# Seven products for both column pairs of a feed-forward down projection, and the squared ReLU moved to ScalarE

## The chip, the core and the metric

The kernel runs on one core of one Trainium2 chip. The metric is the device time of one execution in microseconds (us). It is written in Bass: each engine (TensorE, VectorE, ScalarE, GpSimd, and SyncE, which issues most of the loads) has its own instruction list, worked through strictly in order, and the lists are tied together by semaphores. An instruction that waits holds up everything behind it in its list.

## What is computed

Two layers of an encoder trunk on 256 tokens of width 2048, all in f32. Each layer has a mixing half (an input projection, eight attention heads, a pooling group, an output projection) and a feed-forward half. The change touches the feed-forward half only:

```
x = x + RMSNorm(mix)
f = square(relu(RMSNorm(x) @ w_up)) @ w_down        # 2048 -> 8192 -> 2048
x = x + RMSNorm(f)
```

## The kernel before, in words

**Three products for one.** Every f32 operand is split into a rounded part and a remainder of the type fp32r: `w_hi` is a copy of the weights on ScalarE (`split_hi`, L956), `w_lo` the subtraction raw - w_hi on VectorE (`split_lo`, L1356). A product is then hi*hi + hi*lo + lo*hi, three matmuls of 128x128 weights and 512 columns (function `three`, L847 to L849). SyncE loads 128x1024 pieces of a weight matrix (512 KB each) into the four slots of `raw`; a slot is loaded again once its `w_lo` has been made. The split pieces go into a ring of eight slots, `w_hi` and `w_lo`; a slot is filled again after TensorE has used it (semaphore `w_used`). Four slots are a half, and halves alternate.

**The feed-forward half** works in four groups of 2048 hidden features per layer. A group has four up units (u = 0 to 3) and then the down stage, which adds the group's part to `acc` in two column pairs, j = 0 (output columns 0 to 1023) and j = 1 (the rest). A column pair takes 16 weight pieces in the order `K_ORDER`. Groups 0 to 2 do both pairs in `down_wide`. In the last group j = 0 is done there, and the columns of j = 1 as two plain units, partly loaded into `raw_side`.

**An up unit** leaves its result in `acc_pair[b]` (b = 0, 1), two banks of PSUM each, in which the first 256 columns of a bank hold one partial result and the second 256 another. TensorE works in four quarters: b = 0 and b = 1 on the first half of the weights, then b = 0 and b = 1 on the second, so b = 0 stands a quarter before the unit ends. VectorE adds the partial results with one reduce (L1822) into `act_f`, which frees the banks (semaphore `acc_free[b]`), and makes max(z, 0)*z (L1827). ScalarE copies that to `f_hi` (L1248), VectorE makes `f_lo` (L1833).

**The seven products.** In j = 0, at 4 of the 8 pairs of pieces (`SEVEN_AT`), the 2x2 block product is made with 7 block products instead of 8 (function `seven`, L852). It needs sums of token blocks (`s_sum`, made in up units 1 and 2, split to `s_hi` and `s_lo`), and sums of weight blocks: VectorE makes three into `t_sum` and one in place in `raw` (L1901 to L1913), ScalarE copies `t_hi` (L1263), and VectorE makes `t_lo` (L1917), which lies on the same memory as `t_sum`. So the sums of the next seven wait for `t_used`, which TensorE signals after each of the three products that read `t_hi` and `t_lo`. Three of the seven products go straight to banks of `acc_pair`; four go to banks of their own, the shared banks `ssa_bank`, `t_bank[0]`, `t_bank[1]` and `o_bank`, because they belong to several outputs. One seven is 21 matmuls, and the two plain pieces that follow it are 24. Before the change, the shared banks gather over all four groups of a layer, and `combine` adds them to `acc` in the last group.

**Order of VectorE.** The order is written out by hand. `seven_lo(g, n, ...)` makes the weight sums, two splits, `t_lo`, and two splits more. `wide_sums(g, j)` (L1843, L1846) are four closing sums from the banks of `acc_pair` into `acc`, each of which frees its bank; I call them the closing sums. TensorE starts the next stage when `acc_free` of the bank pair says so. In j = 0 the list is: the last two sevens, two splits of the next stage's first half, the closing sums, then splits. In j = 1 it is: 14 splits (two halves of its own, all of the next stage's first half, two slots of the second), the closing sums, two splits. ScalarE's list has the `w_hi` copies in the same order.

## Time and profile before

| | us |
|---|---|
| median of 3 runs (1904.0 to 1904.77) | 1904.55 |
| span of the profiled execution | 1903.1 |
| TensorE busy (matmul) | 1891.0 (99%) |
| VectorE busy | 1445.1 (76%) |
| ScalarE busy | 983.1 (52%) |
| GpSimd busy | 117.6 (6%) |
| loaded and stored | 380.79 MB, mean 200 GB/s |

The span goes from the first to the last instruction of one execution. The profile gives no other time for that execution; the median of the runs is 1.45 us above its span. The profile names engines PE (TensorE, its matmuls; PEld are its weight loads), DVE (VectorE), ACT (ScalarE), POOL (GpSimd) and SP (SyncE). A line such as `w_lo<-raw,w_hi` reads: writes w_lo, reads raw and w_hi. Matmuls overlap, so the duration of one (380 ns) is longer than the distance from one to the next.

### The profile page before, as it was taken

How to read it: one execution, taken by the hardware profiler on the slowest of the kernel's cores; microseconds unless marked ns; L12 is line 12 of the kernel's file. 1: busy time of each engine (PE TensorE's matmuls, PEld its weight loads, DVE VectorE, ACT ScalarE, POOL GpSimd, SP SyncE). 2: the span in 40 equal slices, each digit the busy share in tenths (PEclk: the TensorE clock that was granted, in tenths of full speed). 3: DMA queues.
4: the chain of work that ended last, by engine and by line, in shares of the span. 5: the costliest groups of instructions: out<-in, count | busy, mean ns of one | idle time of the engine just before them, and what ended most of it. 6: DMA issues, size and time to landing. Idle time of an engine off the chain costs nothing.

```text
span 1903.1 us, 28366 instructions
## 1 busy us (share of the span) xinstructions
PE 1891.0 (99%) x10022; PEld 1685.3 (89%) x10022; DVE 1445.1 (76%) x1777; ACT 983.1 (52%) x1285; POOL 117.6 (6%) x166
## 2 busy tenths in 40 slices
PE   9999999999999999999999999999999999999998
PEld 7988888988988998898888888889889889989987
DVE  6886768886796688579878757678767966876887
ACT  6455656554445445445554556555544544454443
POOL 3920020000000000000000000200000000000000
PEclk9999999999999999999999999999999999999999
DMA  8665356567558557666576554565766575576563
GB/s 290 203 223 173 118 190 218 181 200 241 183 175 262 178 175 227 215 199 187 210 242 220 180 166 138 183 213 169 234 216 200 187 241 187 172 241 209 184 225 149
DMA packets 168325, 380.79 MB, mean 200 GB/s; under 512 B 11968, under 2 KB 14128, under 8 KB 167728
## 3 DMA queue, kind: packets, MB, share of 16 engines
q1 hardware_dynamic: 167904, 377.58, 61.6%
q10 hardware_dynamic: 336, 2.11, 0.3%
q8 instruction: 49, 0.80, 0.2%
q14 instruction: 36, 0.29, 0.0%
HBM read 377.55 MB, written 2.10 MB: 199 GB/s over the span
## 4 chain that ended last, share of the span: by engine, by line
PE 94%; DVE 3%; DMA 1%; issue 1%; ACT 1%; POOL 0%; DVEq 0%; POOLq 0%; ACTq 0%; SPq 0%
PE acc_pair L548 25%; PE acc_pair L553 13%; PE acc_pair L514 8%; PE acc_pair L848 8%; PE acc_pair L516 8%; PE acc_pair L847 8%; PE acc_pair L515 8%; PE acc_pair L849 8%; DVE w_lo L1356 1%; PE o_bank L766 1%; PE t_bank L849 1%; PE t_bank L848 1%; PE t_bank L847 1%; DVE h_both L1410 1%; DMA raw<-in_w_down 0%
## 5 line engine op out<-in xcount | busy, mean ns | idle before, releaser
L1356 DVE TENSOR_TENSOR w_lo<-raw,w_hi 128x1024 fp32r<-128x1024 f32 x687 | 832.3, 1233 | 251.9 <-ACT w_hi L956 243.2
L956 ACT CAST w_hi<-raw 128x1024 fp32r<-128x1024 f32 x687 | 705.5, 1049 | 503.3 <-DVE raw L1904 119.3
L548 PE MATMUL acc_pair<-h_both,w_hi 128*128 128x512 f32 x2176 | 560.2, 380 | 0.1
L548 PEld LDWEIGHTS acc_pair<-h_both,w_hi 128*128 128x128 f32 x2176 | 371.1, 190 | 30.3 <-ACT proj L1025 0.5
L553 PEld LDWEIGHTS acc_pair<-h_both,w_lo 128*128 128x128 f32 x2176 | 327.4, 190 | 29.1
L553 PE MATMUL acc_pair<-h_both,w_lo 128*128 128x256 f32 x2176 | 330.4, 274 | 0.0
L847 PE MATMUL acc_pair<-w_hi,f_hi 128*128 128x512 f32 x672 | 254.7, 379 | 0.0
L848 PE MATMUL acc_pair<-w_lo,f_hi 128*128 128x512 f32 x672 | 254.7, 379 | 0.0
L849 PE MATMUL acc_pair<-w_hi,f_lo 128*128 128x512 f32 x672 | 254.7, 379 | 0.0
L514 PE MATMUL acc_pair<-w_hi,h_both 128*128 128x512 f32 x444 | 170.5, 384 | 1.7 <-DVE w_lo L1356 1.5
L515 PE MATMUL acc_pair<-w_lo,h_both 128*128 128x512 f32 x444 | 168.3, 379 | 0.0
L516 PE MATMUL acc_pair<-w_hi,h_both 128*128 128x512 f32 x444 | 168.3, 379 | 0.0
L514 PE MATMUL acc_pair<-w_hi,f_hi 128*128 128x512 f32 x384 | 148.2, 386 | 0.2
L1248 ACT CAST f_hi<-act_f 128x512 fp32r<-128x512 f32 x60 | 37.1, 619 | 214.1 <-DVE act_f L1827 214.1
L515 PE MATMUL acc_pair<-w_lo,f_hi 128*128 128x512 f32 x384 | 145.5, 379 | 0.0
L516 PE MATMUL acc_pair<-w_hi,f_lo 128*128 128x512 f32 x384 | 145.5, 379 | 0.0
L849 PEld LDWEIGHTS acc_pair<-w_hi,f_lo 128*128 128x128 f32 x672 | 127.0, 189 | 18.1
L848 PEld LDWEIGHTS acc_pair<-w_lo,f_hi 128*128 128x128 f32 x672 | 127.0, 189 | 18.0
L847 PEld LDWEIGHTS acc_pair<-w_hi,f_hi 128*128 128x128 f32 x672 | 127.0, 189 | 18.0
L1822 DVE TENSOR_REDUCE act_f<-acc_pair 128x512 f32<-128x1024 f32 x60 | 73.3, 1221 | 47.1 <-PE acc_pair L553 46.4
L2084 POOL TENSOR_TENSOR rstd<-mean_sq,minus_half 128x1 f32<-128x1 f32 (+1 forms) x16 | 13.5, 843 | 1421.9 <-DVE ss_post L1371 1149.4
L514 PEld LDWEIGHTS acc_pair<-w_hi,h_both 128*128 128x128 f32 x444 | 83.9, 189 | 16.1 <-issue 3.4
(245 smaller groups left out, 1905.4 us busy)
## 6 DMA issues: line engine op xcount, KB each, us to landing
raw<-in_w_up SPq DMA_DIRECT2D x256, 512.0 KB, 4.5
raw<-in_w_down SPq DMA_DIRECT2D x240, 512.0 KB, 4.9
raw<-in_w_in SPq DMA_DIRECT2D x128, 512.0 KB, 4.7
raw<-in_w_out SPq DMA_DIRECT2D x64, 512.0 KB, 5.4
raw_side<-in_w_down SPq DMA_DIRECT2D x16, 512.0 KB, 7.6
x<-in_x SPq DMA_DIRECT2D x8, 256.0 KB, 7.7
w_pool_s<-in_w_pool SPq DMA_DIRECT2D x2, 1024.0 KB, 7.4
post_row<-in_g_mix_post SPq DMA_DIRECT2D x2, 1024.0 KB, 7.4
```

What stands on the lines that cost most here:

```text
L514: pe.matmul(bank[:, :], xh, wh, start=begin and k == 0, stop=False)
L515: pe.matmul(bank[:, :], xh, wl, start=False, stop=False)
L516: mm = pe.matmul(bank[:, :], xl, wh, start=False, stop=end and k == 1)
L548: pe.matmul(acc_pair[b][:, m, :], w_hi[:, slot, col:col + P], x_both.rearrange("p s (a n) -> p s n a", a=2), start=(slot, k) == (0, 0), st ...
L553: mm = pe.matmul(acc_pair[b][:, m, 0:SEQ], w_lo[:, slot, col:col + P], x_hi.rearrange("p (a n) -> p n a", a=2), start=False, stop=(slot, k ...
L847: pe.matmul(bank, xh, in_turn(wh), start=start, stop=False)
L848: pe.matmul(bank, xh, in_turn(wl), start=False, stop=False)
L849: return pe.matmul(bank, xl, in_turn(wh), start=False, stop=stop)
L956: act.copy(w_hi[:, half * PAIRS + p, :], raw[:, p, :]).then_inc(hi_made, 1)
L1248: act.copy(f_part(f_hi, u, b), act_f[:, b, :].rearrange("p (k n) -> p k n", k=2)).then_inc(fhi_made, 1)
L1356: dve.tensor_tensor(w_lo[:, slot, :], src[:, p, :], w_hi[:, slot, :].bitcast(F32), ALU.subtract).then_inc(lo_made, 1)
L1822: dve.tensor_reduce(act_f[:, b, :].rearrange("p (k a n) -> p k a n", k=2, a=2), acc_pair[b][:, :, :].rearrange("p k (s n a) -> p k a n s", ...
```

## The change

In groups 0 to 2, j = 1 also uses seven products in 4 of its 8 pairs of pieces, with the same `K_ORDER` as j = 0. `SHARED` is 4. The shared banks no longer gather over the groups: every column pair starts them anew, and after each pair VectorE takes the four banks into `kept_sums` (`shared_sums`), which lies on the memory of `x`; `x` is therefore written to a tensor in HBM in group 0 and read back in the last group. `combine` is now done once for each j, for j = 1 in the up units of the last group. In the up units ScalarE copies the second halves of the banks to `act_f` (`take_half`), VectorE adds the first halves (`turned_sum`), and ScalarE does Relu, Square and the copy to `f_hi`.

On TensorE:

```diff
+                def bank_free(t, c, j, result):
+                    pe.wait_ge(acc_free[t], result + (c if j else 1))
-                def seven(g, n, hu, result):
+                def seven(g, j, n, hu, result):
-                    pe.wait_ge(flo_made, l * 32 + g * 8 + k1 // 2 + 1)
-                    pe.wait_ge(s_lo_made, no + 1)
+                    if j == 0:
+                        pe.wait_ge(flo_made, l * 32 + g * 8 + k1 // 2 + 1)
+                        pe.wait_ge(s_lo_made, (l * FF_GROUPS + g) * len(SEVEN_AT) + n + 1)
+                    if first and not (isinstance(g, int) and l + g + j == 0):
+                        pe.wait_ge(shared_free, shared_done(l, g, j))
                     pe.wait_ge(lo_made, (hu + i // PAIRS) * PAIRS + 2 + RAW)
                     three(ssa_bank[:, :], sh[:, 2, :], sl[:, 2, :], w_hi[:, s0, right],
-                          w_lo[:, s0, right], p_first, p_last)
+                          w_lo[:, s0, right], first, end)
...
                     for i in range(SLOTS):
-                        slot, kt = i % RING, K_ORDER[j][i]
-                        if j == 0 and i in SEVEN_AT:
-                            seven(g, SEVEN_AT.index(i), hu, result)
-                        if j == 0 and i - i % 2 in SEVEN_AT:
+                        slot, kt = i % RING, K_ORDER[i]
+                        if i in SEVEN_AT:
+                            seven(g, j, SEVEN_AT.index(i), hu, result)
+                        if i - i % 2 in SEVEN_AT:
                             continue
```

On ScalarE:

```diff
+                def take_half(g, u, b):
+                    result_stands(act, b, a0 + ACC_F + g * 8 + u,
+                                  hu0 + HU_F + g * HU_GROUP + u * 2 + 1)
...
+                    act.copy(act_f[:, b, :].rearrange("p (k a n) -> p k a n", k=2, a=2),
+                             acc_pair[b][:, :, SEQ:].rearrange("p k (n a) -> p k a n", a=2)
+                             ).then_inc(half_taken, 1)
                 def turned_hi(g, u, b):
+                    act.wait_ge(acc_free[b], 1 + a0 + ACC_F + g * 8 + u + 1)
+                    act.activation(act_f[:, b, :], act_f[:, b, :], ACT.Relu).then_inc(relu_made, 1)
+                    act.wait_ge(relu_made, turned_no(l, g, u, b) + 1)
+                    act.activation(act_f[:, b, :], act_f[:, b, :], ACT.Square).then_inc(f_ready, 1)
                     act.wait_ge(f_ready, l * 32 + g * 8 + u * 2 + b + 1)
...
+                        act.wait_ge(x_ready, l * 16 + 16)
+                        for t in range(T):
+                            act.dma_start(x_kept[l, t], x[:, t, :]).then_inc(x_saved, 16)
...
+                            if last and u == CHUNKS - 1:
+                                act.wait_ge(q_step, 16 * l + 8)
+                                act.dma_start(x[:, 0, :], x_kept[l, 0]).then_inc(x_back[0], 16)
...
-                    for k, bank in ((0, t_bank[0]), (1, t_bank[1])):
-                        act.copy(halves(q_sum[:, k, :]), put_back(bank[:, :])).then_inc(p_copied, 1)
...
-                    act.wait_ge(q_step, 8 * (l + 1))
+                    act.wait_ge(q_step, 16 * (l + 1))
+                    act.dma_start(x[:, 1, :], x_kept[l, 1]).then_inc(x_back[1], 16)
```

On VectorE:

```diff
-                def turned_square(g, u, b):
-                    dve.tensor_reduce(act_f[:, b, :].rearrange("p (k a n) -> p k a n", k=2, a=2),
-                                      acc_pair[b][:, :, :].rearrange("p k (s n a) -> p k a n s",
-                                                                     s=2, a=2),
-                                      AX.X, ALU.add).then_inc(acc_free[b], 1)
-                    dve.wait_ge(acc_free[b], 1 + a0 + ACC_F + g * 8 + u + 1)
-                    dve.scalar_tensor_tensor(z, z, 0.0, z, ALU.max, ALU.mult
-                                             ).then_inc(f_ready, 1)
+                def turned_sum(g, u, b):
+                    dve.wait_ge(half_taken, turned_no(l, g, u, b) + 1)
+                    z = act_f[:, b, :].rearrange("p (k a n) -> p k a n", k=2, a=2)
+                    dve.tensor_tensor(z, acc_pair[b][:, :, 0:SEQ].rearrange("p k (n a) -> p k a n", a=2),
+                                      z, ALU.add).then_inc(acc_free[b], 1)
+                def f_stands(g, u, b):
+                    dve.wait_ge(f_ready, l * 32 + g * 8 + u * 2 + b + 1)
...
+                    if between is not None:
+                        between()
                     split_lo(hu, half, (2, 3))
...
+                def shared_sums(g, j, first):
+                    if first and j == 0:
+                        dve.wait_ge(x_saved, 16 * T * (l + 1))
+                    dve.wait_ge(t_used, 3 * seven_no(l, g, j, len(SEVEN_AT)) - 1)
+                    for k, bank in enumerate((ssa_bank, t_bank[0], t_bank[1], o_bank)):
+                        dst = kept_sums[:, 1 - j, k, :]
+                        if first:
+                            dve.tensor_copy(dst, bank[:, :]).then_inc(shared_free, 1)
+                        else:
+                            dve.tensor_tensor(dst, bank[:, :], dst, ALU.add
+                                              ).then_inc(shared_free, 1)
...
                 def wide_pair(g, j, first, last=False):
                     hu = hu0 + HU_F + g * HU_GROUP + 2 * CHUNKS + PAIR_HALVES * j
-                    if j == 0:
-                        seven_lo(g, 2, hu + 2, 0)
-                        seven_lo(g, 3, hu + 3, 1)
-                        split_lo(hu + PAIR_HALVES, 0, (0, 1))
+                    seven_lo(g, j, 2, hu + 2, 0)
+                    seven_lo(g, j, 3, hu + 3, 1)
+                    nxt = hu + PAIR_HALVES
+                    if j == 0 and not last:
+                        seven_lo(g, 1, 0, nxt, 0, between=lambda: shared_sums(g, j, first))
                         wide_sums(g, j, first)
-                        split_lo(hu + PAIR_HALVES, 0, (2, 3))
-                        split_lo(hu + PAIR_HALVES + 1, 1, src=raw_side if last else raw)
+                        seven_lo(g, 1, 1, nxt + 1, 1)
+                    elif j == 0:
+                        split_lo(nxt, 0, (0, 1))
+                        shared_sums(g, j, first)
+                        split_lo(nxt, 0, (2,))
+                        wide_sums(g, j, first)
+                        split_lo(nxt, 0, (3,))
+                        split_lo(nxt + 1, 1, src=raw_side)
                     else:
-                        for n in range(PAIR_HALVES - 1):
-                            split_lo(hu + n + 2, n % 2)
-                        split_lo(hu + PAIR_HALVES + 1, 1, (0, 1))
+                        split_lo(nxt, 0)
+                        shared_sums(g, j, first)
+                        split_lo(nxt + 1, 1, (0, 1))
                         wide_sums(g, j, first)
-                        split_lo(hu + PAIR_HALVES + 1, 1, (2, 3))
+                        split_lo(nxt + 1, 1, (2, 3))
...
+                            if last and u < 2:
+                                combine(1, 2 * u)
+                                combine(1, 2 * u + 1)
...
-                        combine(p)
+                        combine(0, p)
```

## Rows read from the trace of the kernel before

**Rows 1.** The page: its head and the first engine of part 1.

```profile
span 1903.1 us, 28366 instructions
PE 1891.0 (99%) x10022; PEld 1685.3 (89%) x10022; DVE 1445.1 (76%) x1777; ACT 983.1 (52%) x1285; POOL 117.6 (6%) x166
```

**Rows 2.** Windows: j = 0, j = 1, up units; length, busy us (count), clock, DMA share, GB/s.

```profile
542.18:581.05 38.87, 38.87 (x183) 34.04 (x182) 34.28 (x37) 21.07 (x21) 0.00 (x0) 1.00 0.61 192
581.05:622.50 41.45, 41.45 (x194) 36.21 (x193) 26.88 (x25) 19.94 (x20) 0.00 (x0) 1.00 0.78 253
...
458.37:542.18 83.81, 83.81 (x513) 76.96 (x513) 63.40 (x77) 36.47 (x40) 0.00 (x0) 1.00 0.60 188
```

**Rows 3.** Timeline of TensorE, second group of layer 0; start us, us, instruction.

```profile
564.63 0.38 PE L849 MATMUL t_bank<-t_hi,s_lo 128*128 128x512 f32 x1
...
571.32 0.38 PE L847 MATMUL ssa_bank<-w_hi,s_hi 128*128 128x512 f32 x1
...
581.04 0.38 PE L847 MATMUL acc_pair<-w_hi,f_hi 128*128 128x512 f32 x1
...
622.48 1.03 PE L548 MATMUL acc_pair<-h_both,w_hi 128*128 128x512 f32 x4
```

**Rows 4.** Timeline of VectorE, same group; in brackets the idle time before.

```profile
549.08 2.36 DVE L1356 TENSOR_TENSOR w_lo<-raw,w_hi 128x1024 fp32r<-128x1024 f32 x2 [0.23 <-ACT w_hi L956]
...
565.16 0.69 DVE L1901 TENSOR_TENSOR t_sum<-raw 128x512 f32<-128x512 f32 x1 [0.44 <-PE t_bank L849]
565.80 0.69 DVE L1904 TENSOR_TENSOR raw<-raw 128x512 f32<-128x512 f32 x1
...
567.77 2.36 DVE L1356 TENSOR_TENSOR w_lo<-raw,w_hi 128x1024 fp32r<-128x1024 f32 x2
570.10 1.76 DVE L1917 TENSOR_TENSOR t_lo<-t_sum,t_hi 128x1536 fp32r<-128x1536 f32 x1
571.77 2.36 DVE L1356 TENSOR_TENSOR w_lo<-raw,w_hi 128x1024 fp32r<-128x1024 f32 x2
...
577.02 1.23 DVE L1356 TENSOR_TENSOR w_lo<-raw,w_hi 128x1024 fp32r<-128x1024 f32 x1 [1.24 <-ACT w_hi L956]
...
620.74 2.73 DVE L1846 SCALAR_TENSOR_TENSOR acc<-acc_pair,rstd,acc 128x512 f32<-128x512 f32 x4 [0.94 <-PE acc_pair L849]
```

**Rows 5.** Timeline of ScalarE, same group, just behind the last seven of j = 0.

```profile
575.94 1.05 ACT L956 CAST w_hi<-raw 128x1024 fp32r<-128x1024 f32 x1 [1.42 <-DMA raw<-in_w_down]
578.80 1.06 ACT L956 CAST w_hi<-raw 128x1024 fp32r<-128x1024 f32 x1 [1.81 <-DMA raw<-in_w_down]
580.06 1.05 ACT L956 CAST w_hi<-raw 128x1024 fp32r<-128x1024 f32 x1 [0.20 <-DMA raw<-in_w_down]
```

**Rows 6.** Groups by line, whole span: count, then busy us, mean ns, idle before.

```profile
L1822 DVE TENSOR_REDUCE act_f<-acc_pair 128x512 f32<-128x1024 f32 x60 | 73.3, 1221 | 47.1 <-PE acc_pair L553 46.4
L1827 DVE SCALAR_TENSOR_TENSOR act_f<-act_f 128x512 f32<-128x512 f32 x60 | 41.5, 692 | 2.1
L1934 DVE TENSOR_TENSOR q_sum<-o_bank,q_sum 128x512 f32<-128x512 f32 x2 | 1.4, 682 | 0.0
L1006 ACT ACTIVATE act_f<-act_f 128x512 f32<-128x512 f32 x4 | 2.5, 631 | 0.1
L1315 ACT COPY q_sum<-t_bank 128x512 f32<-128x512 f32 x4 | 2.1, 582 | 0.0
```

**Rows 7.** Timelines of VectorE and TensorE, last group of layer 0.

```profile
893.32 0.69 DVE L1901 TENSOR_TENSOR t_sum<-raw 128x512 f32<-128x512 f32 x1 [0.86 <-PE t_bank L849]
...
907.14 1.23 DVE L1356 TENSOR_TENSOR w_lo<-raw,w_hi 128x1024 fp32r<-128x1024 f32 x1 [2.92 <-ACT w_hi L956]
...
909.30 0.38 PE L514 MATMUL acc_pair<-w_hi,f_hi 128*128 128x512 f32 x1
```

**Rows 8.** Windows of 1 us at the end of the span, columns as in rows 2.

```profile
1895.00:1896.00 1.00, 0.11 (x1) 0.00 (x0) 0.75 (x1) 0.06 (x1) 0.00 (x0) 1.00 0.00 0
...
1899.00:1900.00 1.00, 0.00 (x0) 0.00 (x0) 1.00 (x2) 0.00 (x0) 0.00 (x0) 0.55 0.89 334
```

More of the change, by code:

```diff
@@ L306, in build @@
     t_hi_made, t_lo_made, t_used = sem("t_hi_made"), sem("t_lo_made"), sem("t_used")
[L307 removed]
+    shared_free, q_step = sem("shared_free"), sem("q_step")
+    x_saved, x_back = sem("x_saved"), [sem(f"x_back{t}") for t in range(T)]
+    half_taken, relu_made = sem("half_taken"), sem("relu_made")
     f_ready, fhi_made, flo_made = sem("f_ready"), sem("fhi_made"), sem("flo_made")
@@ L897, in down_wide @@
                             for c in range(2):
-                                if i == 0:
-                                    pe.wait_ge(acc_free[t], result + c)
-                                begin = i == 0 if j else i == 2 and (t, c) == (1, 1)
+                                begin = i == 2 and (t, c) == (1, 1)
+                                if begin:
+                                    bank_free(t, c, j, result)
                                 mm = three(acc_pair[t][:, c, :], f_hi[:, kt, h_cols(t)],
@@ L1918, in seven_lo @@
                                       ALU.subtract).then_inc(t_lo_made, 1)
+                    if between is not None:
+                        between()
                     split_lo(hu, half, (2, 3))
-                def combine(which):
-                    q1, q5, q6, q7 = (q_sum[:, k, :] for k in range(4))
+                def shared_sums(g, j, first):
[4 more added lines that the diff above has]
+                        dst = kept_sums[:, 1 - j, k, :]
+                        if first:
+                            dve.tensor_copy(dst, bank[:, :]).then_inc(shared_free, 1)
+                        else:
+                            dve.tensor_tensor(dst, bank[:, :], dst, ALU.add
+                                              ).then_inc(shared_free, 1)
@@ L1925, in into, with combine @@
+                def combine(j, which):
+                    q7, q1, q5, q6 = (kept_sums[:, 1 - j, k, :] for k in range(SHARED))
+                    base = 16 * l + 8 * (1 - j)
                     def into(t, c, part):
-                        dst = acc[:, t, c_cols(c)]
-                        dve.scalar_tensor_tensor(dst, part, rstd[:, COL_X2 + t:COL_X2 + t + 1], dst,
+                        dst = halves(acc[:, t, c_cols(2 * j + c)])
+                        dve.scalar_tensor_tensor(dst, put_back(part),
+                                                 rstd[:, COL_X2 + t:COL_X2 + t + 1], dst,
```

124 lines of the change are left out of this document (69 added, 55 removed).

## The prediction

> **What bounds the kernel now.** I began with the page. TensorE is busy for 1891.0 of 1903.1 us [rows 1], so matmuls set the time and whatever makes TensorE wait is added to it. The median of the runs is 1904.55 us, 1.45 us above the span of the profiled execution; I carry that difference along unchanged. A difference of 0.2% (3.8 us) is about what a measurement of this kernel can tell from none.
>
> Next, the stage windows of one middle FFN group [rows 2]. The up units take 83.8 us. The first column pair (j = 0, already with seven products) takes 38.87 us for 180 matmuls and the second (j = 1, plain) 41.45 us for 192, 0.216 us for each. In all three TensorE never idles, while VectorE is busy for 63.4, 34.3 and 26.9 us. The reader is to see two things: the stage that is to be changed is the one where VectorE has most room, and the stage that is its model, j = 0, leaves VectorE 4.6 us in 38.9.
>
> Last, the instructions in time on three engines around the end of j = 0. They show how far VectorE is ahead there. t_lo lies on t_sum, so the next half's sums can't start before TensorE has read t_lo of the half before: that product's last matmul starts at 564.63 [rows 3] and VectorE starts its sums at 565.16, after 0.44 us of idle [rows 4]. This seven starts on TensorE at 571.32 [rows 3], the one before it 45 matmuls (9.72 us) earlier, at 561.60. So the rule for a half is D = S' + 3.55, where S' is the start of the preceding seven on TensorE. From D the two first splits end at 570.13 (D + 4.97), t_lo keeps VectorE until 571.77 (D + 6.61), and the last two splits until about 574.1 (D + 9.0) [rows 4]. Thus at S3, the start of the last seven, VectorE is at D + 6.16 and has 2.8 us of work left, whatever happens before. In a plain half no such link exists: before the change VectorE is a ring ahead at the end of j = 1, and its four closing sums start at 620.74, 0.94 us after waiting for the matmuls themselves; TensorE goes on at 622.48 without a gap [rows 3, 4].
>
> **Removed matmuls.** Four sevens in each of six j = 1 stages (groups 0 to 2, two layers) save 3 matmuls each: 72 x 0.216 = 15.5 us, all on the path. Term: -15.5.
>
> **j = 0 to j = 1, six times.** S3 = 571.32; TensorE could begin j = 1 at S3 + 9.72 = 581.04 [rows 3]. Its first product now waits for all four shared_sums, because the shared banks restart. VectorE prepares the first seven of j = 1 first. D = S3 + 3.55 = 574.87. The second sum needs the second raw slot, whose copy on ScalarE began when it landed, at 575.94 [rows 5]; VectorE starts that sum then. From a second sum to the first split is 567.77 - 565.80 = 1.97 us, to t_lo 4.30 us, and t_lo holds VectorE 1.67 us more [rows 4]: free at 581.88. A sum from PSUM lasts 0.68 us [rows 6] and follows its predecessor by 0.60: the four are done at 584.4, and TensorE starts at 584.5, a stall of 3.5 us. Two splits (2.27 us to the next start) bring VectorE to 586.6; the first closing sum then frees acc_pair[0] at 587.4, but TensorE wants it 6 matmuls after its start, at 585.8: 1.55 us more. The next bank comes 0.66 us later, together with its three matmuls. Term: 6 x 5.05 = 30.3. Without the wait for raw it would be 4.6; no reason makes it less, since D is tied to TensorE.
>
> **j = 1 to the next up units, six times.** Now j = 1 ends at its own S3 + 9.72, and VectorE is at the same D + 9.0 = S3 + 2.8. Ahead of the sums that free acc_pair[0] the code has four splits, the four shared_sums, and two splits. If VectorE alone paces them: 4.6 + 2.4 + 2.3, then 1.4 for both banks, S3 + 13.5 and with signalling 13.7; stall 4.0. But the four raw slots are freed late too: the pattern exists in the trace after j = 0, where ScalarE could copy slots 2 and 3 only at 578.80 and 580.06, D + 14.90 for the last [rows 5]. Its split would start at D + 16.05 and end its hold at D + 17.15 = S3 + 11.0. Then 2.4 + 2.3 + 1.4 and signalling: S3 + 17.2, a stall of 7.5 us. I take 7.5, as those loads are the same size and are released in the same order. Term: 6 x 7.5 = 45.0. Lower end 4.0; upper end by the pacing of the last group, where the split of its second slot began at 907.14, 13.8 us after D = 893.32 [rows 7], against 577.02, 11.9 us after D, in the middle group [rows 4]: 2 us later; over four slots I allow 3.3 more, 10.8.
>
> **TensorE's clock.** At the end of the trace TensorE's work ends at 1895.1, and the granted clock of the stretch from 1899 to 1900 is 0.55, full for its first tenth and half from then on [rows 8]. It fell from 2.4 to 1.2 GHz some 4.0 us after work ended. A stall of 7.5 us is longer, so I expect six falls; the stalls of 3.5 and 1.55 us are shorter. No row has TensorE working at the lower level, so the price is bounded: nothing if the clock returns at once, 5.2 us if the first quarter of an up unit (a sixteenth of 83.8 us [rows 2]) runs at half rate. I take 2.0, half of the 4.0 us that the fall took. Term: 12.0.
>
> **The up units.** Removed from VectorE: a reduce of 1221 ns and a max-square of 692 ns; added to it one sum of 0.68 us. Added to ScalarE: copy 0.58, Relu 0.63, Square 0.63 [rows 6], eight times a group in 83.8 us in which it is busy for 36.5 [rows 2]. Behind the half copy in its queue are w_hi copies; a half slot is due only 10.5 us after the unit's end, and the half copy, sum and signals free acc_pair[1] about 2 us after that end, due at 5.2 us. So nothing in units 0 to 2. In unit 3 the chain after the last result is 0.58 + 0.68 + 0.63 + 0.63 with four signals, 2.75, against 1.22 + 0.69 and two, 2.0. The second seven's preparation slides by 0.8 us; its splits were done at 549.08 + 2.36 = 551.44 [rows 4] and TensorE needs them at 542.18 + 9.72 = 551.90: 0.35 us of stall. Term: 8 x 0.35 = 2.8 (0 to 8).
>
> **Last groups, twice.** Four shared_sums (2.4 us) and one split (1.1) now precede the first closing sum. Before, it came right behind the split at 907.14 and ended at 907.14 + 1.13 + 0.75 = 909.0, for a start of TensorE at 909.30 [rows 7]. Now it ends at 909.0 + 2.4 + 1.13 = 912.55, with a signal 3.3 late, 0.5 of it regained since small later waits vanish. Term: 2 x 2.8 = 5.6.
>
> **At nothing:** combine(1), eight instructions in two up units of a group, covered by 20 us of VectorE idle per group [rows 2] (5.3 us a layer if that cover were gone). The copies of x: 2.1 MB out and back per layer on ScalarE's queue, while weights take 0.60 of the DMA engines; filled raw slots and ring cover them. Uncovered, each would cost 2.1 MB at 253 GB/s, 8.3 us, four times. The issues are behind waits that are long met; the bank copies of L1315 go.
>
> **Sum:** -15.5 + 30.3 + 45.0 + 12.0 + 2.8 + 5.6 = +80.2; 1903.1 + 80.2 + 1.45 = 1984.7 us. The likeliest case's own range is 1970 to 2000.
>
> **Rivals.**
> (a) VectorE alone paces both boundaries, and the clock stays up: -15.5 + 6 x (4.6 + 4.0) + 2.8 + 5.6 = +44.5, 1949. For it: DMA has room on average. Against: slots 2 and 3 did land late [rows 5]. 26%.
> (b) Loads as slow as in the last group, 2.0 and 3.3 us more per boundary: 2016. 12%.
> (c) The clock falls at the j = 0 to j = 1 boundary as well, two short stalls with 1.3 us of work between: another 6 x 2.0, 1996.7. For it: total idle is 5.05; against: the one fall took 4.0 us. 10%. The Trainium skill, TensorE: Matmul & The Clock Gate, section "HAM oscillation — how this bites in real kernels", describes a kernel that waits for data before every tile and is dropped to the slow clock every time; by that rule each of the twelve stalls may count, while the trace of this case has only one fall.
> (d) Faster: VectorE keeps its lead, so that no boundary stalls, and only removed matmuls and the 2.8 remain: 1891.9. Place: the closing sums of j = 1. It decides if VectorE's preparation of the last seven ends 4 us earlier than S3 + 2.8. The link at 565.16 speaks against it. 5%.
> (e) Stalls small enough to cancel 15.5: 2%.
> (f) ScalarE's longer chain frees acc_pair[1] late in the up units: 1 us in each of 30 would add 30, 2015; its 3 us of room speak against. 3%.
> Left unsaved, the matmuls would show in TensorE's count of 10022; nothing in the diff suggests that.
>
> **Numbers.** The forecast has 42%. Slower 93%, same 2%, faster 5%. The range 1944 to 2010 takes in (a), (c) and most of the forecast's bounds and leaves out (b), (d), (e) and (f), about 2 in 10 with the edges.
>
> **What would show it.** TensorE's count down by 72. Idle of TensorE before the first ssa_bank product of j = 1, released by shared_sums, near 3.5 us, and before the first up matmul, released by a closing sum, near 7.5; VectorE starting each seven's sums right after a t_bank product. ScalarE's w_hi waiting for raw there. A clock of half for some us after the long stall. If TensorE's busy share stays at 99%, the forecast is wrong; if the long stall is near 4 us, rival (a) holds.

## The result, and the profile after

The changed kernel takes 1976.11 us (median of 4 runs, 1973.5 to 1978.15) against 1904.66 us (4 runs, 1904.0 to 1905.59): ratio 1.0373, 95% interval 1.0358 to 1.0387. It is slower. The forecast was 1984.7 us with a range of 1944 to 2010, so it is 8.6 us above the median. The profiled execution took 1973.5 us, its span is 1971.0, 67.9 us above the span of before.

The page of the changed kernel, its head and the start of its chain of waits (against [rows 1]; in the chain of before TensorE had 94%, VectorE 3%):

```profile
span 1971.0 us, 28901 instructions
PE 1893.9 (96%) x9950; PEld 1681.8 (85%) x9950; DVE 1518.0 (77%) x1909; ACT 1111.8 (56%) x1485; POOL 117.8 (6%) x166
...
PE 80%; DVE 10%; DMA 4%; issue 4%; ACT 2%; DVEq 0%; POOL 0%; ACTq 0%; SPq 0%; POOLq 0%
```

TensorE has 72 matmuls fewer, yet is busy for 2.9 us more: some of them ran at half clock. The rest of the loss is waiting. The largest waits of TensorE in the changed kernel (us in total, times, longest):

```profile
PE acc_pair L563 <- DVE acc L1895: 25.1, 4, 6.9
PE ssa_bank L862 <- DVE kept_sums L1982: 11.8, 4, 3.0
PE acc_pair L563 <- DVE acc L1892: 11.5, 2, 6.1
PE ssa_bank L862 <- DVE kept_sums L1980: 5.2, 2, 2.6
PE acc_pair L529 <- DVE acc L1895: 4.2, 2, 2.2
PE acc_pair L862 <- DVE acc L1895: 3.8, 3, 1.3
PE acc_pair L862 <- DVE acc L1892: 2.7, 2, 1.4
```

L563 is the first product of the up units. L862 is the first of the three matmuls of a product in j = 0 or j = 1; when it writes ssa_bank, a seven begins. L529 is the first matmul of a product in a plain unit, here of the units that follow j = 0 in a last group. L1895 and L1892 are the closing sums, L1982 and L1980 the shared sums (the second of each pair in a layer's first group). TensorE's instructions in time, around both boundaries of the second group of layer 0 (start, us, then in brackets the idle time before and what ended it), which stand against [rows 3]:

```profile
581.62 0.38 PE L862 MATMUL ssa_bank<-w_hi,s_hi 128*128 128x512 f32 x1
...
594.40 0.48 PE L862 MATMUL ssa_bank<-w_hi,s_hi 128*128 128x512 f32 x1 [2.90 <-DVE kept_sums L1982]
...
597.24 0.48 PE L862 MATMUL acc_pair<-w_hi,f_hi 128*128 128x512 f32 x1 [1.28 <-DVE acc L1895]
...
634.70 0.38 PE L864 MATMUL acc_pair<-w_hi,f_lo 128*128 128x512 f32 x1
641.93 2.07 PE L563 MATMUL acc_pair<-h_both,w_hi 128*128 128x512 f32 x4 [6.86 <-DVE acc L1895]
```

S3 of j = 0 is 581.62. TensorE could have begun j = 1 9.72 us later, at 591.34; it began at 594.40. VectorE in the same time, against [rows 4]:

```profile
585.18 0.69 DVE L1950 TENSOR_TENSOR t_sum<-raw 128x512 f32<-128x512 f32 x1 [0.32 <-PE t_bank L864]
585.80 0.70 DVE L1953 TENSOR_TENSOR raw<-raw 128x512 f32<-128x512 f32 x1
...
590.11 1.76 DVE L1966 TENSOR_TENSOR t_lo<-t_sum,t_hi 128x1536 fp32r<-128x1536 f32 x1
591.78 0.68 DVE L1982 TENSOR_TENSOR kept_sums<-ssa_bank,kept_sums 128x512 f32<-128x512 f32 x1
...
594.17 2.35 DVE L1405 TENSOR_TENSOR w_lo<-raw,w_hi 128x1024 fp32r<-128x1024 f32 x2
596.44 2.72 DVE L1895 SCALAR_TENSOR_TENSOR acc<-acc_pair,rstd,acc 128x512 f32<-128x512 f32 x4
...
619.04 0.69 DVE L1950 TENSOR_TENSOR t_sum<-raw 128x512 f32<-128x512 f32 x1 [0.78 <-PE t_bank L864]
...
632.72 1.22 DVE L1405 TENSOR_TENSOR w_lo<-raw,w_hi 128x1024 fp32r<-128x1024 f32 x1 [0.93 <-ACT w_hi L978]
634.49 1.23 DVE L1405 TENSOR_TENSOR w_lo<-raw,w_hi 128x1024 fp32r<-128x1024 f32 x1 [0.55 <-ACT w_hi L978]
635.64 0.68 DVE L1982 TENSOR_TENSOR kept_sums<-ssa_bank,kept_sums 128x512 f32<-128x512 f32 x1
...
638.03 2.35 DVE L1405 TENSOR_TENSOR w_lo<-raw,w_hi 128x1024 fp32r<-128x1024 f32 x2
640.30 2.71 DVE L1895 SCALAR_TENSOR_TENSOR acc<-acc_pair,rstd,acc 128x512 f32<-128x512 f32 x4
```

The link is there: D = 585.18 = 581.62 + 3.56, released by a product of t_bank. Everything behind it is in code order, without a gap until the shared sums. TensorE's wait ends only when the four shared sums have ended, and the next wait when two splits and the first closing sum have. At the end of j = 1 VectorE is D + 15.45 = 634.49 into its list when it starts the last split of the next half, and still has four shared sums and two splits ahead of the closing sums. ScalarE makes the copy that this last split needs at 633.41, after waiting for the load (against the last of [rows 5]):

```profile
633.41 1.04 ACT L978 CAST w_hi<-raw 128x1024 fp32r<-128x1024 f32 x1 [0.72 <-DMA raw<-in_w_up]
```

Windows of that long wait in the changed kernel (stretch, length, busy us and count of PE, PEld, DVE, ACT, POOL, then the granted clock, DMA share, GB/s), and of the up units behind it:

```profile
634.90:636.90 2.00, 0.18 (x1) 0.00 (x0) 2.00 (x4) 1.02 (x2) 0.00 (x0) 1.00 0.89 287
636.90:637.90 1.00, 0.00 (x0) 0.00 (x0) 1.00 (x3) 0.87 (x1) 0.00 (x0) 0.67 0.81 260
637.90:641.90 4.00, 0.00 (x0) 0.00 (x0) 4.00 (x6) 2.09 (x2) 0.00 (x0) 0.50 0.61 173
641.90:646.90 5.00, 4.96 (x15) 4.25 (x16) 3.38 (x4) 0.00 (x0) 0.00 (x0) 0.50 0.73 235
646.90:647.90 1.00, 1.00 (x6) 0.95 (x6) 0.00 (x0) 0.00 (x0) 0.00 (x0) 0.71 1.07 381
...
641.93:728.56 86.63, 86.62 (x512) 79.45 (x513) 55.88 (x70) 47.46 (x60) 0.00 (x0) 0.97 0.59 191
```

The clock falls from 2.4 to 1.2 GHz a third of a microsecond into the second window, about 637.2, when TensorE has been idle for 2.2 us (its last matmul began at 634.70 and lasted 0.38), and returns at about 647.5. TensorE works for 5.5 us of that at half rate, which costs half of it, 2.8: 86.63 us for the up units instead of 83.84 [rows 2]. This is the longest of the six; at the other five the low stretch lasts 6.8 us and costs 1.6 to 2.1.

To see where all of the 67.9 us came from I took, from TensorE's timeline, the start of every seven and of every stage. Undisturbed, sevens start 9.72 us apart.

| place (times) | intervals measured, us | excess, sum | predicted |
|---|---|---|---|
| matmuls, 9950 for 10022 | | -15.5 | -15.5 |
| last seven of j = 0 to first of j = 1 (6) | 12.45 to 12.92 | 17.9 | 21.0 |
| first to second seven of j = 1 (6) | 11.37 to 11.46 | 10.1 | 9.3 |
| last seven of j = 1 to the up units (6) | 15.34 to 16.73 | 37.5 | 45.0 |
| up units, 83.84 before (6) | 85.46 to 86.63 | 11.9 | 12.0 |
| up units to the first sevens (8) | two of 9.8 each | 1.5 | 2.8 |
| last seven to the plain units, last groups (2) | 12.11 and 11.85 | 4.5 | 5.6 |
| sum | | +67.9 | +80.2 |

The difference of the two spans is 67.9 us as well.

### The profile page after: what moved, and what is told of

Same layout as the page of the kernel before. It is cut to its first block, busy times and chain, and to the rows that moved or that the text cites. A ratio compares the mean times of both kernels' runs of the same rounds, so it can differ in the third digit from the quotient of the medians.

```text
span 1971.0 us, 28901 instructions
## 1 busy us (share of the span) xinstructions
PE 1893.9 (96%) x9950; PEld 1681.8 (85%) x9950; DVE 1518.0 (77%) x1909; ACT 1111.8 (56%) x1485; POOL 117.8 (6%) x166
## 4 chain that ended last, share of the span: by engine, by line
PE 80%; DVE 10%; DMA 4%; issue 4%; ACT 2%; DVEq 0%; POOL 0%; ACTq 0%; SPq 0%; POOLq 0%
PE acc_pair L563 24%; PE acc_pair L568 12%; PE acc_pair L529 8%; PE acc_pair L530 8%; PE acc_pair L531 8%; DVE w_lo L1405 5%; PE acc_pair L862 4%; PE acc_pair L864 4%; PE acc_pair L863 4%; DMA raw<-in_w_down 2%; DMA raw<-in_w_up 2%; ACT w_hi L978 1%; PE t_bank L864 1%; PE t_bank L862 1%; PE t_bank L863 1%
## 5 line engine op out<-in xcount | busy, mean ns | idle before, releaser
L563 PE MATMUL acc_pair<-h_both,w_hi 128*128 128x512 f32 x2176 | 569.9, 385 | 36.7 <-DVE acc L1895 25.1
L563 PEld LDWEIGHTS acc_pair<-h_both,w_hi 128*128 128x128 f32 x2176 | 377.1, 194 | 69.6 <-issue 39.0
L862 PE MATMUL acc_pair<-w_hi,f_hi 128*128 128x512 f32 x504 | 192.0, 381 | 6.6 <-DVE acc L1895 3.8
L863 PE MATMUL acc_pair<-w_lo,f_hi 128*128 128x512 f32 x504 | 191.3, 380 | 0.0
L864 PE MATMUL acc_pair<-w_hi,f_lo 128*128 128x512 f32 x504 | 191.3, 380 | 0.0
L529 PE MATMUL acc_pair<-w_hi,h_both 128*128 128x512 f32 x444 | 170.7, 385 | 2.3 <-DVE w_lo L1405 1.7
L529 PE MATMUL acc_pair<-w_hi,f_hi 128*128 128x512 f32 x384 | 148.4, 386 | 4.2 <-DVE acc L1895 4.2
L531 PE MATMUL acc_pair<-w_hi,f_lo 128*128 128x512 f32 x384 | 145.7, 380 | 0.0
L530 PE MATMUL acc_pair<-w_lo,f_hi 128*128 128x512 f32 x384 | 145.7, 380 | 0.0
L862 PEld LDWEIGHTS acc_pair<-w_hi,f_hi 128*128 128x128 f32 x504 | 95.5, 189 | 22.4 <-DVE acc L1895 5.7
L1872 DVE TENSOR_TENSOR act_f<-acc_pair,act_f 128x512 f32<-128x512 f32 x60 | 41.5, 692 | 87.0 <-ACT act_f L1275 84.8
L864 PEld LDWEIGHTS acc_pair<-w_hi,f_lo 128*128 128x128 f32 x504 | 95.5, 189 | 13.3
L863 PEld LDWEIGHTS acc_pair<-w_lo,f_hi 128*128 128x128 f32 x504 | 95.5, 189 | 13.2
L1275 ACT COPY act_f<-acc_pair 128x512 f32<-128x512 f32 x60 | 35.0, 583 | 119.6 <-PE acc_pair L568 119.6
L529 PEld LDWEIGHTS acc_pair<-w_hi,h_both 128*128 128x128 f32 x444 | 84.1, 189 | 16.8 <-issue 3.7
```

The costliest lines, as they stand in the source:

```text
L529: pe.matmul(bank[:, :], xh, wh, start=begin and k == 0, stop=False)
L530: pe.matmul(bank[:, :], xh, wl, start=False, stop=False)
L531: mm = pe.matmul(bank[:, :], xl, wh, start=False, stop=end and k == 1)
L563: pe.matmul(acc_pair[b][:, m, :], w_hi[:, slot, col:col + P], x_both.rearrange("p s (a n) -> p s n a", a=2), start=(slot, k) == (0, 0), st ...
L862: pe.matmul(bank, xh, in_turn(wh), start=start, stop=False)
L863: pe.matmul(bank, xh, in_turn(wl), start=False, stop=False)
```

## Experiments

Nine more kernels ran. In all of them "before" is the kernel before on the same chip, and medians are compared. The expectations use other names for some of them: e7 is experiment 6, e9 experiment 8.

### 1. The up units alone

The kernel before with the new up units and nothing else: ScalarE copies the second halves, VectorE adds, ScalarE does maximum and square. In short:

```diff
-  dve.tensor_reduce(z, acc_pair[b], AX.X, ALU.add)          # VectorE
-  dve.scalar_tensor_tensor(z, z, 0.0, z, ALU.max, ALU.mult) # VectorE
+  act.copy(z, acc_pair[b][:, :, SEQ:])                      # ScalarE
+  dve.tensor_tensor(z, acc_pair[b][:, :, 0:SEQ], z, ALU.add)
+  act.activation(z, z, ACT.Relu); act.activation(z, z, ACT.Square)
```

> The kernel before with only the change of the up units (ScalarE copies the second halves, Relu, Square; VectorE adds). Theory, order of VectorE at the stage boundaries: this part costs only the later preparation of the second seven, about 0.2 us in each of 8 groups: 1.5 us, ratio 1.0008. Rival, the ScalarE chain holds up the up units: several us, 1910 or more, with TensorE waiting for acc_free inside the up units. Rival, the move gives VectorE time that is worth something: faster by 2 us or more.

Measured: 1907.12 us (10 runs) against 1905.03 (14), ratio 1.0009 (0.9999 to 1.0019); span 1905.1. The sevens after the up units start 9.83 and 9.79 us apart, as in the changed kernel, and no wait of TensorE lies inside the units. So this part costs about 2 us (from nothing to 3.6 by the interval), and rival (f), ScalarE's chain holding acc_pair[1], is out. ScalarE's chain in the changed kernel, in time, shows the latency that was added:

```profile
552.50 0.58 ACT L1275 COPY act_f<-acc_pair 128x512 f32<-128x512 f32 x1 [1.95 <-PE acc_pair L568]
553.84 0.63 ACT L1282 ACTIVATE act_f<-act_f 128x512 f32<-128x512 f32 x1 [0.76 <-DVE act_f L1872]
554.50 0.63 ACT L1284 ACTIVATE act_f<-act_f 128x512 f32<-128x512 f32 x1
```

### 2. Closing sums first at the end of j = 1

The changed kernel; only the order of VectorE's list behind the last seven of j = 1 is another. Two splits and then the closing sums is the order that the kernel before has behind j = 0; the shared sums wait until nobody needs them soon.

```diff
-                        split_lo(nxt, 0)
-                        shared_sums(g, j, first)
-                        split_lo(nxt + 1, 1, (0, 1))
-                        wide_sums(g, j, first)
-                        split_lo(nxt + 1, 1, (2, 3))
+                        split_lo(nxt, 0, (0, 1))
+                        wide_sums(g, j, first)
+                        split_lo(nxt, 0, (2, 3))
+                        split_lo(nxt + 1, 1)
+                        shared_sums(g, j, first)
```

> The changed kernel, with the closing sums of j = 1 put behind two splits of the next half, and shared_sums put last. Theory: the stall before the next up units (37.5 us in all) shrinks to about 0.3 us each and the six falls of the clock (12 us) go: 1976 - 36 - 12 = 1928 us; the stalls between j = 0 and j = 1 stay at 28 us. Rival, the loads pace this boundary: the stall moves to the first up matmuls, which wait for w_lo, and less than half of it goes, 1950 or more. Rival, VectorE has more work than time in a seven stage: the stalls reappear inside the sevens and the time stays near 1970.

Measured: 1930.62 us, ratio 1.0134 (1.0117 to 1.0151), span 1927.5: 43.5 less than the changed kernel. VectorE and TensorE of this kernel in time, at the same boundary:

```profile
627.23 2.73 DVE L1895 SCALAR_TENSOR_TENSOR acc<-acc_pair,rstd,acc 128x512 f32<-128x512 f32 x4 [1.74 <-PE acc_pair L864]
```

```profile
628.97 1.03 PE L563 MATMUL acc_pair<-h_both,w_hi 128*128 128x512 f32 x4
```

Now VectorE waits 1.74 us for the matmuls and TensorE goes on without a gap. The interval is 9.71 or 9.72 us at all six places, and the up units take 83.84 us again: the long stall and its clock falls, 49.4 us, went with this change of order alone, every engine's work being the same. Some 6 of them came back. The j = 0 to j = 1 boundaries took 4.6 us more, since the clock now fell at five of the six, where it had fallen at one, and the last groups 2.4 us more, with one fall behind layer 1's last j = 0. Windows of this kernel, around that boundary in the same group:

```profile
587.00:589.00 2.00, 1.43 (x4) 0.61 (x2) 2.00 (x4) 0.00 (x0) 0.00 (x0) 0.50 0.33 61
589.00:593.00 4.00, 3.99 (x9) 3.16 (x10) 1.93 (x3) 0.00 (x0) 0.00 (x0) 0.50 0.70 231
```

### 3. The other boundary: shared sums in pieces

The changed kernel; behind the last seven of j = 0 the shared sums of ssa_bank and t_bank[0] come before the next seven's sums, those of t_bank[1] and o_bank and the closing sum of t = 0 ahead of t_lo, and TensorE waits for each bank by itself.

```diff
-                        seven_lo(g, 1, 0, nxt, 0, between=lambda: shared_sums(g, j, first))
-                        wide_sums(g, j, first)
+                        shared_sums(g, j, first, (0, 1))
+
+                        def early():
+                            shared_sums(g, j, first, (2, 3))
+                            wide_sums(g, j, first, (0,))
+
+                        seven_lo(g, 1, 0, nxt, 0, between=lambda: wide_sums(g, j, first, (1,)),
+                                 early=early)
```

> The changed kernel, with shared_sums between j = 0 and j = 1 taken in two pieces (ssa_bank and t_bank 0 ahead of the weight sums, the others behind the first two splits), the closing sums of t = 0 ahead of t_lo, and TensorE waiting for each shared bank by itself. Theory: the stalls of 4.67 us at this boundary shrink to about 0.7 us each, 6 x 4 = 24 us off: 1952 us; the long stalls and the clock falls stay. Rival, the seven's preparation is too long in any order: over 3 us of stall stays at each boundary, 1965 or more.

Measured: 1971.27 us, ratio 1.0339 (1.0322 to 1.0356), span 1968.7. A miss: 2.3 us less in the spans, 4.8 in the medians, instead of 24. The wait ahead of the first seven went, as meant (9.71 us). But the next interval grew to between 11.59 and 12.26 us, TensorE waiting for t_lo and splits instead, and the end of j = 1 slipped by 0.6 us each. Waits of TensorE in this kernel:

```profile
PE acc_pair L563 <- DVE acc L1901: 26.4, 4, 7.3
PE acc_pair L563 <- DVE acc L1898: 13.6, 2, 7.3
PE acc_pair L529 <- DVE acc L1901: 4.8, 2, 2.7
PE t_bank L862 <- DVE t_lo L1974: 4.5, 6, 0.8
PE ssa_bank L862 <- DVE w_lo L1411: 3.6, 8, 0.5
```

The excess at this boundary and in the sevens behind it fell from 28.0 to 15.1 us. Most of that was lost again elsewhere: 3.6 us in the longer stalls at the end of j = 1, 3.4 us in the up units, where the clock falls cost 15.3 us instead of 11.9, and 3.9 us in the last groups, at both of which the clock now fell as well. So this order pays about half of VectorE's debt at the boundary, 13 us of the 24 expected, and 11 went again at the later stalls. Why those grew I did not test.

### 4. All orders

Experiments 2 and 3 together, and in the last groups the closing sums ahead of the shared sums.

```diff
                         split_lo(nxt, 0, (0, 1))
-                        shared_sums(g, j, first)
-                        split_lo(nxt, 0, (2,))
                         wide_sums(g, j, first)
-                        split_lo(nxt, 0, (3,))
+                        split_lo(nxt, 0, (2, 3))
                         split_lo(nxt + 1, 1, src=raw_side)
+                        shared_sums(g, j, first)
```

> The changed kernel with both new orders and, in the last group, the closing sums ahead of shared_sums. Theory: of the stalls only 6 x (0.7 + 0.3) and the 1.5 us of the up units stay and the removed matmuls show: 1904.6 - 15.5 + 6 + 1.5 = 1897 us, no clock fall. Rival, VectorE's work per seven stage (43 us of instructions against 38.9 us of matmuls) is itself the bound: above 1915 us, with TensorE waiting for w_lo or t_lo inside the sevens.

Measured: 1912.58 us, ratio 1.0037 (1.0023 to 1.0051), span 1910.1, between the two numbers. The clock stays up throughout (0.999). What is left is the interval from the first to the second seven of j = 1, 11.92 to 12.62 us: 14.7 us over its six places, in several short waits. They nearly equal the 15.5 us that the removed matmuls save. The span is 7.0 us above that of before, for the rest adds to it: 2.7 us in the last groups, 2.2 in the intervals behind the up units, 1.9 in one stage of up units that waited 1.0 us for act_f, 0.7 between the other sevens. With four sevens in j = 1, the best order that I found still leaves the kernel slower than before.

```profile
PE t_bank L862 <- DVE t_lo L1974: 4.8, 6, 0.8
PE ssa_bank L862 <- DVE w_lo L1411: 3.6, 8, 0.5
```

### 5. Shared sums later, the rest as changed

The changed kernel; only the shared sums of j = 1 go behind the last splits. It asks what those four instructions alone cost.

```diff
                         split_lo(nxt, 0)
-                        shared_sums(g, j, first)
                         split_lo(nxt + 1, 1, (0, 1))
                         wide_sums(g, j, first)
                         split_lo(nxt + 1, 1, (2, 3))
+                        shared_sums(g, j, first)
```

> The changed kernel with one step moved: in j = 1 the four shared_sums stand behind the closing sums and the last splits instead of ahead of them. Theory, VectorE's list in series sets the stall before the up units: each of the six shrinks by the four sums, 2.4 us, from 6.3 to 3.9 us, 14.4 us in all; the idle time is still longer than the 2.4 to 3.4 us after which the clock fell in the changed kernel, so the falls stay: 1976 - 14.4 = 1962 us. Rival, the loads end last: the splits of the second half wait for raw instead, and less than 1 us of each stall goes, 1970 or more. Third outcome, the clock no longer falls: another 12 us less, 1950.

Measured: 1971.68 us (1966.26 to 1978.26), ratio 1.0354 (1.0331 to 1.0377), span 1969.4. A miss: 1.6 us less in the spans, 4.4 in the medians, instead of 14. The stall did shrink, from 6.3 to 4.9 us, 8.0 in all; it gave back 1.3 us of the 2.4 that the shared sums last. Between D and the closing sums VectorE now waits for loads and ScalarE's copies for 3.0 us on average, against 2.2 in the changed kernel; in four of the six groups 0.8 to 1.1 us of that is at the two splits of the second half, which now come that much earlier and find their copies not yet made. VectorE of this kernel in time:

```profile
634.70 3.85 DVE L1405 TENSOR_TENSOR w_lo<-raw,w_hi 128x1024 fp32r<-128x1024 f32 x3 [1.03 <-ACT w_hi L978]
```

And the clock took the rest: the shorter stall was still long enough for six falls (up units 85.55 to 86.74 us, 3.5 more in sum), and it now fell at all six j = 0 to j = 1 boundaries (2.3 more) and once in a last group (1.9 more). So both bounds of the third term hold together here: VectorE's list, and the loads close behind it.

### 6. Three sevens in j = 1

The version that the first four pointed to. If VectorE lacks about 2.5 us ahead of the second seven of j = 1, one seven less there gives it a seven's sums and t_lo, some 4.3 us, and ten more microseconds until shared banks restart. The first pair of j = 1 is plain; the shared sums slip between the first splits. Behind j = 1 stands the order of experiment 2; in the last groups the shared sums follow the first split and the closing sums the second. It saves 54 matmuls instead of 72.

```diff
-                    first, end = n == 0, n == len(SEVEN_AT) - 1
+                    first, end = n == j, n == len(SEVEN_AT) - 1
...
-                        if i in SEVEN_AT:
+                        at = SEVEN_AT[j:]
+                        if i in at:
...
-                        seven_lo(g, 1, 0, nxt, 0, between=lambda: shared_sums(g, j, first))
+                        split_lo(nxt, 0, (0,))
+                        shared_sums(g, j, first, (0, 1))
+                        split_lo(nxt, 0, (1,))
+                        shared_sums(g, j, first, (2, 3))
                         wide_sums(g, j, first)
+                        split_lo(nxt, 0, (2, 3))
                         seven_lo(g, 1, 1, nxt + 1, 1)
```

> j = 1 with seven products at three of its eight pairs of pieces instead of four (the first pair is plain), shared_sums between the first splits in VectorE's idle time at both kinds of boundary of j = 0, and the order of the second experiment behind j = 1. 54 matmuls fewer than before, 11.7 us. Theory, what is left over in the fourth experiment (2.2 to 2.9 us in the first seven of each j = 1) is VectorE having ten sums and a seven's preparation in the same ten microseconds; with a plain first pair it fits: 1904.6 - 11.7 + 1.5 (up units) + about 2 = 1896.5 us. Rival, any shared sums and sevens in j = 1 cost TensorE more than they save: 1905 or more.

Measured: 1894.61 us (1894.16 to 1895.12) against 1904.59, ratio 0.9948 (0.9934 to 0.9962), span 1892.0. It is 0.5% faster than the kernel before, and the interval leaves no doubt of the sign. The page's row of engines and the largest waits of TensorE:

```profile
PE 1880.4 (99%) x9968; PEld 1674.1 (88%) x9968; DVE 1489.7 (79%) x1879; ACT 1106.3 (58%) x1479; POOL 117.7 (6%) x166
```

```profile
PE o_bank L610 <- POOL ident L2196: 1.8, 1, 1.8
PE acc_pair L530 <- DVE w_lo L1409: 1.2, 3, 0.4
```

No wait at either boundary is left. VectorE in time shows why:

```profile
577.59 2.71 DVE L1899 SCALAR_TENSOR_TENSOR acc<-acc_pair,rstd,acc 128x512 f32<-128x512 f32 x4
580.22 2.35 DVE L1409 TENSOR_TENSOR w_lo<-raw,w_hi 128x1024 fp32r<-128x1024 f32 x2
...
592.91 0.69 DVE L1954 TENSOR_TENSOR t_sum<-raw 128x512 f32<-128x512 f32 x1 [1.51 <-PE t_bank L865]
```

The closing sums follow the shared sums without a seven's preparation between them, and by 592.91 VectorE is ahead again and idles for 1.51 us before TensorE lets go of t_lo. The saving is 54 x 0.216 = 11.7 us, of which 11.1 arrive in the span. This kernel differs from experiment 4 in the number of sevens and in the order of the sums at once; I did not run them apart.

### 7. Three sevens with the old up units

Experiment 6 with the up units of before. In short:

```diff
-  dve.tensor_tensor(z, acc_pair[b][:, :, 0:SEQ], z, ALU.add)
+  dve.tensor_reduce(z, acc_pair[b], AX.X, ALU.add)
+  dve.scalar_tensor_tensor(z, z, 0.0, z, ALU.max, ALU.mult)
```

> The kernel of e7 with the up units as before the change (reduce and max-square on VectorE). Theory, the up units' part costs 0.2 us per group and brings nothing, since VectorE has over 20 us of idle time in four up units: 1.5 us less than e7, 1895 us. Rival, the time that the move frees on VectorE is needed now that combine and more sums are there: slower than e7, above 1898.

Measured: 1894.95 us (1893.62 to 1897.51), ratio 0.9947 (0.9934 to 0.9961). It can't be told from experiment 6, so the ScalarE part of the change is worth nothing measurable here, in either direction. The intervals behind the up units go back to 9.71 in groups 0 to 2 (9.86 and 9.93 in the last groups), but the profiled execution (span 1894.9) waited for VectorE's squares once:

```profile
PE acc_pair L564 <- DVE act_f L1857: 1.6, 1, 1.6
```

### 8. Shared sums before all splits

A control: the same four instructions moved forward, not back.

```diff
+                        shared_sums(g, j, first)
                         split_lo(nxt, 0)
-                        shared_sums(g, j, first)
                         split_lo(nxt + 1, 1, (0, 1))
```

> The changed kernel with shared_sums of j = 1 ahead of all splits of the next half; control for the next run. The sums wait for the last seven's products, so VectorE loses another 1 to 2 us: stalls before the up units of 6.3 to 8 us, the clock falls at each. 1976 to 1990 us.

Measured: 1989.78 us, ratio 1.0448 (1.0429 to 1.0466), span 1985.5, inside what was expected. The last seven of j = 1 to the up units takes 16.87 to 17.44 us, a stall of 7.5, and the up units lose 16.5 us to the clock over the six. With experiments 2 and 5 that makes four orders of the same four sums, each with a stall of its own: 7.5 us (first of all), 6.3 (as changed), 4.9 (behind everything else), and none once the closing sums are moved ahead too.

### 9. Filler for the clock

Experiment 8 with 26 matmuls of 128x512 in each of the six waits. They go to o_bank once its sums are taken, and nothing reads them; the kernel's own work is complete.

```diff
                         down_wide(g, 1, hu + 2 * CHUNKS + PAIR_HALVES, r + CHUNKS + 2)
+                        pe.wait_ge(shared_free, shared_done(l, g, 1) + SHARED)
+                        for _ in range(26):
+                            pe.matmul(o_bank[:, :].rearrange("p (s n) -> p s n", s=2),
+                                      h_both[:, 0, 0, 0:P], h_both[:, 1, :, :],
+                                      start=True, stop=True)
```

> The kernel of e9 with 26 more matmuls (5.6 us) for TensorE in each of the six waits before the up units, into o_bank, whose sum has been taken; nobody reads their result. Theory, the clock falls because TensorE idles, and each fall costs 2 us of the up units on top of the stall: with the wait filled the clock stays at 2.4 GHz there, the up units take 83.8 us again, and the kernel is 10 to 12 us faster than e9 although it does 156 matmuls more. Rival, the slow start of the up units has another cause, or a gap this short is not what lowers the clock: same time as e9, or slower if the filler outlasts the wait.

Measured: 1981.26 us, ratio 1.0393 (1.0376 to 1.0411), span 1981.6: with 156 matmuls more the kernel is 8.5 us faster than experiment 8. In the profiled executions the up units take 83.93 us three times and 85.6 three times, 10.9 us less in sum; the intervals to them are 0.6 us longer each, 3.5 in sum. The spans differ by only 3.9 us, as this execution also lost some 3 us elsewhere: 1.3 at the ends of the last groups, 1.2 in the stages between the layers, 0.6 ahead of one seven. TensorE's last idle time before the up units in the second group:

```profile
643.75 1.28 PE L563 MATMUL acc_pair<-h_both,w_hi 128*128 128x512 f32 x4 [2.31 <-DVE acc L1900]
```

The filler left 1.5 to 2.3 us of idle time in the six waits. The clock fell at the three longest (1.99, 2.27 and 2.31 us) and not at the three shortest (1.49, 1.80 and 1.92). So the clock's part of the loss is a consequence of TensorE's idling, which work without use can reduce. It is no repair: the stall itself stays.

## Why the prediction was right, and where its steps were off

**What bounds it.** Right. The path went from TensorE's queue to VectorE's list, ordered by D = S' + 3.55: D was at S3 + 3.56 in the changed kernel. Experiment 2 shows by the order alone that VectorE's list makes the stall.

**Removed matmuls.** Exactly 72, -15.5 us.

**j = 0 to j = 1.** Predicted 3.5 and 1.55 us, measured 2.7 to 3.2 and 1.65 to 1.74, a sum of 28.0 for 30.3. The step that was off is the wait of the second sum for its raw slot: it started at 585.80, 0.62 us behind the first, with no wait. That weight came sooner than in the row that I took. The end "without the wait for raw", 4.6 a boundary, is what happened (4.67).

**j = 1 to the up units.** The largest miss: 37.5 us for 45.0. The mechanism stands; the step that was mis-sized is what the late loads add. I took it whole from where slots 2 and 3 were copied after a j = 0, D + 14.90. Here the last of them came at 633.41, D + 14.4, in the slowest of the six groups, and the shared sums began at D + 16.6, not 17.15. In that group VectorE waited 0.62 us for a load ahead of its second sum and 0.70, 0.93 and 0.55 us for ScalarE's copies, 2.8 of a stall of 7.01. The other five groups waited 1.7 to 2.3 us and stalled for 5.6 to 6.3. Taking these waits off leaves 4.0 to 4.3 us in each of the six, an estimate: VectorE's own list makes the 4.0 of rival (a), and the loads add 2.2 on average where the forecast had 3.5. So the truth lay between the forecast and rival (a), nearer to the forecast. Experiment 5 bears it out from the other side: with 2.4 us of sums taken off VectorE's list, only 1.3 came back.

**The clock.** 12.0 predicted, 11.9 measured. All six falls came, at a cost of 1.6 to 2.8 us each. The size is right by luck: I had taken half of the 4.0 us after which the clock fell at the end of the trace, and that is no measure of how long TensorE then works at half rate. In the long stalls it fell 2.2 to 3.2 us after the last matmul (the expectation of experiment 5 says 2.4 to 3.4), and stayed low for 6.8 us, once 10.2. Rival (c), falls at the first boundary too, happened at one of six places in the changed kernel and cost little. The Trainium skill, TensorE: Matmul & The Clock Gate, section "HAM oscillation — how this bites in real kernels", describes a kernel whose waits of about 3 to 5 us each cost the fast clock. The changed kernel's trace agrees at all six long stalls, 5.5 to 6.9 us of idle time. The short ones, 2.6 to 3.0 us, are at the lower edge of the page's waits or below it, and there the traces give no rule: one fall in six places here, five in experiment 2, six in experiment 5, four in experiment 8, one in experiment 9.

**Up units.** 1.5 us for 2.8, and nothing that a measurement can tell (experiments 1 and 7). The chain was as long as assumed, 2.63 us from the copy's start to the end of Square against 2.75. What was too large is the part of it that reaches TensorE: 0.1 us at each of the two sevens behind the units, not 0.35.

**Last groups.** 4.5 us for 5.6. The interval is back at 9.71 us in both last groups of experiment 4, with the closing sums first, and of experiment 6, with the shared sums and two splits ahead of them instead of three.

**At nothing.** The copies of x went as assumed: no wait of TensorE names them. On the page, among the DMA issues, their median from issue to landing is 7.2 and 5.9 us:

```profile
x_kept<-x ACTq DMA_DIRECT2D x4, 1024.0 KB, 7.2
x<-x_kept ACTq DMA_DIRECT2D x4, 1024.0 KB, 5.9
```

Combine(1) in the up units of a last group made no wait either.

**Rival (d)**, faster through a kept lead, needed VectorE 4 us earlier. Nothing in the changed kernel gave it that. Experiment 2 has no stall at the end of j = 1, by the order alone; experiment 6 has none at either boundary, with one seven less besides.

## What to carry to other kernels

Trading matmuls for work on another engine pays only while that engine's list, between the points where it is tied to TensorE's progress, is shorter than TensorE's time there; a mean busy share of 76% said nothing on this, one timeline between two such ties did. When an accumulator is wanted back at once, the sums that free it belong first in the queue, and evictions that nobody waits for belong behind them: here that order alone was worth 43 us (experiment 2). If one more seven (or any such saving) makes a debt, try one fewer before giving the whole up: three sevens of four kept 54 of the 72 matmuls' saving, and that version (experiments 6 and 7) is the only one here that gained.

## What I had not expected of the hardware

One fall of the clock, read at the end of a trace, is no measure of when it falls elsewhere. It came 4.0 us after the last matmul of the kernel before [rows 8], 2.0 us after that of the changed kernel, and from 2.0 to 5.1 us after that of the others. In the changed kernel's long stalls it came after 2.2 to 3.2 us, in those of experiment 3, which are about as long, after 4.5 to 5.1. After a fall it stayed at 1.2 GHz while TensorE was already working, 3.1 to 5.5 us long; this, and not the idle time, is what it costs. It can even come when TensorE is at work again: in three of experiment 2's five falls at the short stalls, 0.2 to 0.7 us after the first matmul, and in all three before experiment 9's up units, 0.8 to 1.0 us after.

Waits of nearly the same length had different fates. The idle time of 2.6 to 3.0 us ahead of the first seven of j = 1 brought a fall at one of six places in the changed kernel, at five of six in experiment 2 (2.6 to 3.4 us), and at all six in experiment 5. In experiment 9 a wait of 3.3 us at that place brought none, and one of 2.0 us before the up units did. What makes the difference I did not settle. It has a consequence for measuring: runs of experiment 5 spread over 12 us, the mean granted clock being 0.986 in the fastest and 0.982 in the slowest, and those of the changed kernel over 4.7. Those of the kernel before and of experiment 6, at 0.999, spread over 1.6 and 1.0 us. The clock is not the only source of spread: experiment 7 has 0.999 too and spreads over 3.9.
